# Sparse attention of a hybrid decoder layer: all heads of a query block in turn, logits from 64 rows, division once a block

## The reference

```
h = h + 0.5 * swiglu(rmsnorm(h), ffn1)
h = h + [GLA(4 heads) | sparse attention(8 heads of 64)] @ w_out      # on rmsnorm(h) @ w_in
h = h + 0.5 * swiglu(rmsnorm(h), ffn2)
out = rmsnorm(h)[:, 16:]
```

```
logits = q . k / 8, over the selected keys that are visible, else -inf
p      = softmax(logits)
out    = p @ v                                    # per head
```

## Time and profile before

| | us |
|---|---|
| median of 3 runs | 1195.07 (1193.54 to 1195.66) |
| the profiled execution: its time | 1195.07 |
| the profiled execution: its span | 1195.1 |
| TensorE busy in it | 1147.0 (96%) |
| attention, first logits to first projection matmul | 687.9 to 769.6 |

### The profile page before, as it was taken

The page is one execution under the profiler, slowest core; times in us unless marked ns, Lnnn a source line. Parts: engine busy times, 40 slices in busy tenths (PEclk is TensorE's granted clock), DMA queues, the critical chain, the costliest instruction groups (busy, mean ns, idle before and its releaser), DMA issues.

```text
span 1195.1 us, 19518 instructions
## 1 busy us (share of the span) xinstructions
PE 1147.0 (96%) x7331; PEld 1021.1 (85%) x7331; DVE 620.5 (52%) x989; ACT 359.0 (30%) x547; POOL 508.0 (43%) x283
## 2 busy tenths in 40 slices
PE   6999999999999999995789999999999999999997
PEld 6999999999999996895787777887887888788886
DVE  5644123531346955996996466555542144512556
ACT  5422112221222342621122356533221122212223
POOL 2634444444433635246746150045444444444442
PEclk8999999999999999997989899999999999999999
DMA  5423332333321444132312000033333333333311
GB/s 179 124 88 89 90 93 83 103 90 88 88 70 54 124 129 112 47 105 57 96 36 71 19 1 1 17 89 100 110 89 88 106 88 88 106 88 88 88 53 71
DMA packets 175545, 98.70 MB, mean 83 GB/s; under 512 B 6019, under 2 KB 169910, under 8 KB 175494
## 3 DMA queue, kind: packets, MB, share of 16 engines
q1 hardware_dynamic: 175494, 98.02, 28.5%
HBM read 91.18 MB, written 2.10 MB: 78 GB/s over the span
## 4 chain that ended last, share of the span: by engine, by line
PE 85%; DVE 7%; issue 5%; ACT 1%; POOL 1%; DVEq 0%; POOLq 0%; ACTq 0%
PE ps L1538 70%; PE ps L371 5%; PE ps L540 3%; PE ps L550 2%; PE ps L567 2%; DVE mask L857 1%; PE ps L525 1%; DVE ikga L904 1%; DVE iq L926 1%; POOL wl L1192 1%; PE ps L462 1%; DVE small L853 1%; DVE gb L882 0%; DVE t L904 0%; PE ps L513 0%
## 5 line engine op out<-in xcount | busy, mean ns | idle before, releaser
L1192 POOL TENSOR_TENSOR wl<-raw,wh 128x1024 fp32r<-128x1024 f32 x173 | 429.7, 2486 | 614.0 <-ACT wh L1327 613.8
L1538 PE MATMUL ps<-xh,wh 128*128 128x264 f32 (+2 forms) x1392 | 354.0, 315 | 6.1 <-DVE xl L1436 5.6
L1538 PE MATMUL ps<-xl,wh 128*128 128x264 f32 (+2 forms) x1392 | 353.6, 315 | 0.0
L1538 PE MATMUL ps<-xh,wl 128*128 128x264 f32 (+2 forms) x1392 | 352.2, 314 | 0.0
L1327 ACT ACTIVATE wh<-raw 128x1024 fp32r<-128x1024 f32 x173 | 181.3, 1052 | 289.8 <-PE ps L1538 278.7
L1538 PEld LDWEIGHTS ps<-xh,wh 128*128 128x128 f32 (+1 forms) x1392 | 230.2, 190 | 23.4 <-issue 7.2
L1538 PEld LDWEIGHTS ps<-xl,wh 128*128 128x128 f32 (+1 forms) x1392 | 229.6, 190 | 15.7 <-issue 0.2
L1538 PEld LDWEIGHTS ps<-xh,wl 128*128 128x128 f32 (+1 forms) x1392 | 229.4, 190 | 14.8
L1538 PE MATMUL ps<-ah,wh 128*128 128x264 f32 (+1 forms) x592 | 166.8, 330 | 0.0
L1538 PE MATMUL ps<-al,wh 128*128 128x264 f32 (+1 forms) x592 | 166.4, 330 | 0.0
L1538 PE MATMUL ps<-ah,wl 128*128 128x264 f32 (+1 forms) x592 | 166.1, 329 | 0.0
(11 more groups left out here) (210 smaller groups left out, 1067.0 us busy)
## 6 DMA issues: line engine op xcount, KB each, us to landing
raw<-in_ffn_w_gate SPq DMA_DIRECT2D x44, 512.0 KB, 3.7
raw<-in_ffn_w_up SPq DMA_DIRECT2D x44, 512.0 KB, 3.7
raw<-in_ffn_w_down SPq DMA_DIRECT2D x32, 512.0 KB, 3.8
raw<-in_w_in SPq DMA_DIRECT2D x28, 512.0 KB, 3.7
raw<-in_ffn_w_down SPq DMA_DIRECT2D x16, 384.0 KB, 3.3
raw<-in_w_out SPq DMA_DIRECT2D x8, 512.0 KB, 3.9
sw<-pjb SPq DMA_DIRECT2D x32, 66.0 KB, 2.0
xin<-in_x SPq DMA_DIRECT2D x4, 512.0 KB, 4.2
```

Of the source, the lines that this page charges most:

```text
L1192: pool.tensor_tensor(wl[:, slot, :], raw[:, slot, :], wh[:, slot, :].bitcast(F32), ALU.subtract).then_inc(w_split, 1)
L1538: mm = pe.matmul(ps[0:m, bank + a, 0:width], w[:, slot, k * P:k * P + m], r[:, tiles[k], t:t + width], start=(k == 0 and n == 0), stop=(k ...
```

## The change

- The order of the steps: block 4 first, then 3, 2, 1, 0, all eight heads of a block in turn, written out without a loop (`ATT_ORDER`, `TURNS`).
- Logits: queries and keys are read where the projection left them (`pjb`), 64 rows, even heads on partitions 0 to 63, odd heads on 64 to 127. From step 8 on, those of two steps are issued one after the other. GpSimd's zeroing and its copies (`stage`) go.
- Probabilities: exponential in place in `lg` (four buffers instead of two), without a sum; `dg` and `inverse` go. They are turned by plain transposes against the identity, and copied by VectorE (even steps) or ScalarE (odd steps), in one instruction.
- Values: the turned probabilities are the weights, and a head's 64 value columns with a column of ones, 65, move. The result has queries on partitions and the sum of the exponentials beside them. All eight heads of a block gather in two banks.
- Once a block (`scale_out`): a reciprocal of eight sums and one multiply; TensorE transposes the four tiles back (`turn_out`, after the fourth step of the next block), ScalarE and VectorE split them in `ah` and `al`.
- `values` run two steps behind.

```diff
         def att_step(n):
-            pair, rest = divmod(n, 2 * len(BLK))
-            e, rest = divmod(rest, len(BLK))
-            b = ATT_ORDER[rest]
-            return (pair, e, b) + BLK[b]
+            b = ATT_ORDER[n // HEADS]
+            return (b, n % HEADS) + BLK[b]
+        def qk_bank(n):
+            return 2 * (n % 2) if n < HEADS else n % 4
+        TURNS = []
+        for n_head in range(N_ATT):
+            TURNS.append((True, n_head))
+            if n_head % HEADS == 3 and n_head > HEADS:
+                TURNS.append((False, n_head // HEADS - 1))
+        TURNS.append((False, len(BLK) - 1))
+        def keep_probs(eng, n):
+            b, hd, s, w = att_step(n)
+            t = TURNS.index((True, n))
+            eng.wait_ge(p_turned, n + 1)
+            if n >= 3:
+                eng.wait_ge(pv_done, n - 2)
+            src, dst = ps[:, 4 + t % 2, 0:(b + 1) * w], pt[:, n % 3, 0:(b + 1) * w]
+            if by_dve(n):
+                eng.tensor_copy(dst, src).then_inc(pt_dve, 1)
+            else:
+                eng.activation(dst, src, ACT.Copy).then_inc(pt_act, 1)
@@ TensorE
-            pe.wait_ge(kst_zero, 4)
+            def logits(n):
+                b, hd, s, w = att_step(n)
+                pair, e = hd // 2, HD * (hd % 2)
+                for a, (k0, kn) in enumerate(key_parts(b)):
+                    mm = pe.matmul(ps[0:w, qk_bank(n) + a, 0:kn], pjb[e:e + HD, pair, s:s + w],
+                                   pjb[e:e + HD, 4 + pair, k0:k0 + kn], start=True, stop=True)
+                mm.then_inc(qk_done, 1)
+            def turn_probs(n, t):
+                b, hd, s, w = att_step(n)
+                pe.wait_ge(exp_done, n + 1)
+                if t >= 2:
+                    turn_free(pe, t - 2)
+                for c in range(b + 1):
+                    sc, wc = BLK[c]
+                    mm = pe.transpose(ps[0:wc, 4 + t % 2, c * w:(c + 1) * w], lg[0:w, n % 4, sc:sc + wc],
+                                      ident[0:w, 0:w])
+                mm.then_inc(p_turned, 1)
+            def values(n):
+                b, hd, s, w = att_step(n)
+                probs_kept(pe, n)
+                if hd == 0 and n:
+                    pe.wait_ge(o_scaled, n // HEADS)
+                c0 = (hd % 4) * (HD + 1)
+                for c in range(b + 1):
+                    wc = BLK[c][1]
+                    mm = pe.matmul(ps[0:w, 6 + hd // 4, c0:c0 + HD + 1], pt[0:wc, n % 3, c * w:(c + 1) * w],
+                                   dv_heads[0:wc, c, hd, :], start=(c == 0), stop=(c == b))
+                mm.then_inc(pv_done, 1)
+            def turn_out(i, t):
+                s, w = BLK[ATT_ORDER[i]]
+                pe.wait_ge(o_scaled, i + 1)
+                turn_free(pe, t - 2)
+                for j in range(4):
+                    mm = pe.transpose(ps[:, 4 + t % 2, j * w:(j + 1) * w], onat[0:w, j * P:(j + 1) * P],
+                                      ident[0:w, 0:w])
+                mm.then_inc(n_turned, 1)
+            logits(0)
+            pe.wait_ge(o_normed, 1)
+            logits(1)
+            for t, (is_head, n) in enumerate(TURNS):
+                if not is_head:
+                    if n == len(BLK) - 1:
+                        values(N_ATT - 2)
+                        values(N_ATT - 1)
+                    turn_out(n, t)
+                    continue
+                if n + 2 < HEADS:
+                    pe.wait_ge(lg_done, n + 1)
+                    logits(n + 2)
+                elif n % 2 == 0 and n + 2 < N_ATT:
+                    pe.wait_ge(lg_done, n + 1 if n + 2 == HEADS else n)
+                    logits(n + 2)
+                    if n + 2 == HEADS:
+                        pe.wait_ge(lg_done, n + 2)
+                    logits(n + 3)
+                if n == 0:
+                    pe.wait_ge(o_normed, len(WIN))
+                turn_probs(n, t)
+                if n >= 2:
+                    values(n - 2)
@@ VectorE
+            def scale_out(i):
+                s, w = BLK[ATT_ORDER[i]]
+                o = ps[0:w, 6:8, 0:4 * (HD + 1)].rearrange("p a (h d) -> p a h d", d=HD + 1)
+                r = rinv[0:w, :].rearrange("p (a h) -> p a h", a=2)
+                dve.wait_ge(pv_done, HEADS * (i + 1))
+                dve.reciprocal(r.unsqueeze(3), o[:, :, :, HD:HD + 1]).then_inc(sum_inv, 1)
+                if i:
+                    dve.wait_ge(n_turned, i)
+                dve.wait_ge(sum_inv, i + 1)
+                dve.tensor_tensor(onat[0:w, :].rearrange("p (a h d) -> p a h d", a=2, d=HD), o[:, :, :, 0:HD],
+                                  r.unsqueeze(3).broadcast_to([w, 2, 4, HD]), ALU.mult).then_inc(o_scaled, 1)
+            for is_head, n in TURNS:
+                if is_head:
+                    if n + 2 < N_ATT:
+                        masked(n + 2)
+                    if by_dve(n):
+                        keep_probs(dve, n)
+                    if n % HEADS == 1 and n > HEADS:
+                        scale_out(n // HEADS - 1)
...
@@ ScalarE: the exponential of the next step, then the copy of an odd step, or the outputs' high half
+            for is_head, n in TURNS:
+                if is_head:
+                    if n + 1 < N_ATT:
+                        probs(n + 1)
+                    if not by_dve(n):
+                        keep_probs(act, n)
...
@@ GpSimd
+            pool.memset(dv_heads[:, :, :, HD:HD + 1], 1.0).then_inc(dv_ones, 1)
-            for n, (pair, e) in enumerate(((0, 0), (0, 1), (1, 0), (1, 1))):
-                pool.memset(kst[pair][e][64 * (1 - e):64 * (1 - e) + HD, :], 0.0).then_inc(kst_zero, 1)
-            stage(0)
-            stage(1)
...
-            stage(2)
-            stage(3)
```

More of the change, by code:

```diff
@@ L154, in build @@
         pjb = sb("pjb", [P, 8, TOK])
-        dv = sb("dv", [P, 5, 512])
+        dv = sb("dv", [P, 5, HEADS * (HD + 1)])
         mask = sb("mask", [P, sum(SEEN)])
@@ L531, in pe_mixer @@
             pe.wait_ge(s_new, GLA_HEADS * FULL_WIN)
-            pe.wait_ge(kst_zero, 4)
[L533 to L548, removed]
-                        wc = BLK[c][1]
-                        mm = pe.matmul(ps[HD * e:HD * (e + 1), 6 + n % 2, 0:w], vst[pair][0:wc, c, HD * e:HD * (e + 1)],
-                                       pt[0:wc, n % 2, c * w:(c + 1) * w], start=(c == 0), stop=(c == b))
-                    mm.then_inc(pv_done, 1)
-                logits(0)
-                logits(1)
-                for n in range(N_ATT):
-                    pair, e, b, s, w = att_step(n)
-                    if n + 2 < N_ATT:
-                        logits(n + 2)
-                    if n == 0:
-                        pe.wait_ge(o_normed, len(WIN))
-                    pe.wait_ge(diag_done, at(i, N_ATT, n + 3))
-                    pe.wait_ge(pt_kept, at(i, N_ATT, n + 1))
-                    for c in range(b + 1):
-                        sc, wc = BLK[c]
-                        mm = pe.matmul(ps[0:wc, 4 + n % 2, c * w:(c + 1) * w], pr[0:w, n % 2, sc:sc + wc],
-                                       dg[0:w, n % 2, 0:w], start=True, stop=True)
-                    mm.then_inc(pt_done, 1)
-                    if n:
-                        values(n - 1)
-                values(N_ATT - 1)
@@ new lines, in masked @@
+            def masked(n):
+                b, hd, s, w = att_step(n)
+                dve.wait_ge(qk_done, n + 1)
+                if n >= 4:
+                    dve.wait_ge(p_turned, n - 3)
+                src = ps[0:w, qk_bank(n), 0:SEEN[b]] if SEEN[b] <= 512 else ps[0:w, qk_bank(n):qk_bank(n) + 2, 0:HALF]
+                dve.tensor_tensor_reduce(out=key_view(lg[0:w, n % 4, 0:SEEN[b]], b), in0=src,
+                                         in1=key_view(mask[0:w, MASK_AT[b]:MASK_AT[b] + SEEN[b]], b), scale=-HD ** -0.5,
+                                         scalar=3.0e38, op0=ALU.add, op1=ALU.min,
+                                         accum_out=stat[0:w, n % 4:n % 4 + 1]).then_inc(lg_done, 1)
@@ L1408, in _ @@
             dve.memset(scrap[:, :], 0.0).then_inc(scrap_done, 1)
-            for free in (up_scaled, lg_done, pt_kept, m_lo, diag_done, pv_done):
-                dve.sem_inc(free, 2)
+            dve.sem_inc(up_scaled, 2)
             dve.sem_inc(top_taken, 2)
```

174 lines of the change are left out of this document (56 added, 118 removed).

## The result

The changed kernel takes 1215.63 us (median of 4 runs, 1212.94 to 1220.19) against 1195.37 of the kernel before on the same chip (4 runs, 1193.54 to 1195.78): ratio 1.0181, 95% interval 1.0156 to 1.0207. It is slower; the forecast was 1187.4, faster, with a range of 1183.0 to 1192.5. The profiled execution is the 1212.94 one, with a span of 1211.1.

What follows compares the result with a forecast made beforehand. The prediction took TensorE to bound the kernel: 69.1 us of passes + 1.6 waits + 1.45 tail + 1.8 start = 74.0 against 81.7 for the stage, 7.7 less, so 1195.1 became 1187.4 us, range 1183.0 to 1192.5.

Steps and rivals of the forecast that it cites:

- Start: Attention stage's start: clock at 0.50 until about 691 us loses 1.6 us, with 0.15 of waiting 1.8.
- rival 3: Attention stage: clock sinks to 0.50 because of transposes or 64-row work; low throughout adds 69 us; chance 0.04.
- Turning: Transposes of the probabilities: two passes a chunk, 2.71 us a head, 21.7 for eight; no gain from being transposes.
- Values: Values matmuls: passes priced by their weights, 0.089 us each (0.114 for 128 columns), 21.8 us in all.
- rival 5: Values matmuls priced by their 65 moving columns: 8.4 us less, total 1179; chance 0.05.
- Pairs: Logits from block 3 on: two heads issued together cost as one, 7.3 us; up to 7.3 more otherwise.
- Rival 1: Paired logits overlap not at all or only half: 3.7 or 7.3 us more, 1191 or 1194.6; chance 0.14.
- Switches: Shape changes around 64-row logits: 0.15 + 0.18 us each time in and out, 23 times, 7.6 us.
- Rival 2: Each change between transpose and plain matmul costs 0.16 us, some 56 times: 9 us more, 1196.3; chance 0.06.
- Waits: TensorE stalls at block edges for the division and the outputs' bank, in blocks 1 and 0: 1.6 us together.
- tail: Stage's end, from last turning through last values and division: TensorE idle 1.4 to 1.45 us.
- rival 4: Blocks 1 and 0 become bound by the latency chain: 0.25 us a step in 16 steps, 1191; chance 0.09.

Runs made afterwards that it cites:

- e11: Changed kernel with zero-padded 128-row logits in block 4 alone, 64-row pairs from block 3 on: 1173.27 us, ratio 0.9826.
- e1: Changed kernel with logits over all 128 rows, summing the two heads of a pair (not the reference's numbers): 1177.67 us.
- e5: Kernel before with 64-row logits, nothing else changed: 1272.48 us.
- e14: Changed kernel with 60 transposes of 128x128 put ahead of the first logits: 1223.57 us.
- e6: Kernel before with the probabilities turned by plain transposes, division by the sum left out: 1184.06 us.
- e13: Changed kernel with every transpose of the probabilities issued twice: 1236.25 us.
- e2: Changed kernel with the probabilities turned by plain matmuls against the identity, two passes each: 1202.86 us.
- e10: e8 timed again, 64-row logits always in pairs and 100 moving columns in the values: 1174.16 us, ratio 0.9832.
- e4: Changed kernel with 20 full matmuls (128 rows, 512 columns) put ahead of the first logits: 1218.45 us.
- e7: Changed kernel with logits over 128 rows by zero-padded queries, one copy a head filled by GpSimd: 1171.86 us.
- e9: e7 timed again, changed kernel with zero-padded 128-row logits: 1172.69 us, ratio 0.9819.
- e3: Changed kernel with 128 instead of 65 moving columns in the values: 1192.60 us.
- e8: Changed kernel with 64-row logits always in interleaved pairs, block 4 too, and 100 moving columns in the values: 1176.43 us.
- e15: Changed kernel with 60 transposes of 100x100 put ahead of the first logits: 1225.07 us.

## Why the prediction was wrong

**The step that failed** is the clock of the stage. In the sum it is the term Start: 1.6 us lost, and the clock 1.00 "from about 691"; all of the 69.1 us of passes is priced at full clock. The other way stood there as rival 3, "the clock sinks to 0.50 within the stage because of transposes or of 64-row work", and got 0.04. The runs showed 0.50 from the stage's first instruction to its last, 102.45 us for the 74.0 of the forecast, and with it a sign that the prediction had named, 0.50 after 695 us. Against e11, which differs in block 4's padding alone, the low clock costs 102.45 - 59.98 = 42.5 us. I had the decisive row in hand: the spreading matmuls, 20 rows each, keep TensorE busy 8.41 of 8.70 us at 0.50, while full-row logits see it rise. I read it as a delay of 3 us, not as a property of the work that follows. And the row that made the chance so small, the transposes at the kernel's start, says nothing of 64 rows, and what decides first is the logits' rows (e1, e5). The transposes are not out of it: they raise the clock by themselves (e14) and leave it up beside full rows (e6), but beside 64 rows they didn't bring it up where plain matmuls did (e13, e2).

Rival 3's price, "low throughout adds 69", was too high. Some 14 of the 69.1 are passes that take less than priced (below), and a pass takes not twice as long at half clock but 1.9 times: ten of the values 1.61 us for 0.85. The rest I have not taken apart.

**Turning: mis-sized.** I priced a plain transpose at two passes, because the rows of the kernel before show a matmul as two records and I carried that over. The earlier trace rows had the answer: L1613 and L1633 are x16 for 16 transposes of 128x128. At full clock e11's chain, below, shows five chunks in 0.43 us, 0.087 each, so a head takes 14 x 0.087 + 0.11 = 1.3, eight heads 10.6 instead of 21.7; the outputs' transposes take 0.35 a block instead of 0.71. That is 13 us in the kernel's favour.

The chain of e11, a head of block 4 and a pair in block 3:

```profile
702.63 0.43 PE ps L551 x5
...
703.91 0.90 PE ps L540 x4
704.81 0.49 PE ps L551 x4
705.30 0.85 PE ps L563 x10
706.16 0.35 PE ps L551 x4
706.51 0.85 PE ps L563 x10
```

**Values: right.** 0.85 for ten passes is 0.085 each (forecast 0.089), not the 0.054 of 65 moving columns (rival 5): e10's 100 columns take 1.67 where 65 take 1.61, both at half clock.

**Pairs: right.** 0.90 us for two heads with 428 columns, where one takes 0.89. Rival 1 falls.

**Switches: right.** 0.49 for the first four transposes behind a pair of logits, 0.35 for the next four: 0.14 on that side (forecast 0.15), and the 0.90 is the 0.706 of the columns and 0.19 (forecast 0.18). Between transposes and values there is nothing: 0.35 and 0.85 are the passes alone. Rival 2 falls.

**Waits: right in size.** In e11, at full clock but for its start and end, TensorE idles 59.98 - 57.42 = 2.56 us; forecast 1.6 at block edges and 1.45 in the tail. What its matmuls waited for in e11 (engine, line, what it waited for: us, times, longest), L572 being the outputs' transposes, L563 the values and L551 the transposes of the probabilities:

```profile
PE ps L572 <- DVE onat L1074: 1.1, 1, 1.1
PE ps L563 <- DVE onat L1074: 0.8, 2, 0.5
PE ps L551 <- DVE al L1093: 0.4, 1, 0.4
```

The 0.8 for the multiply at two block edges is the 0.25 and 0.55 of the forecast. No matmul is down as waiting for a mask, an exponential or a copy of probabilities, where rival 4 had 0.25 a step in 16 steps: it falls. In the changed kernel, at half clock, VectorE waits 42.3 us for the logits. What the forecast lacks is the wait for the first mask, 0.92 us where the stage starts at full clock (e4).

The wait in the tail can cost more than its 1.1 us. In e11 the clock falls behind it, and the projection starts at half clock (first row: the stretch behind the wait). In e7 the same wait is there and the clock stays up (second row).

```profile
743.70:747.00 3.30, 3.30 (x10) 2.76 (x11) 0.69 (x1) 1.54 (x2) 0.67 (x1) 0.50 0.03 5
```

```profile
744.60:748.00 3.40, 3.40 (x17) 2.72 (x16) 0.69 (x1) 1.55 (x2) 1.73 (x1) 1.00 0.00 0
```

Of the traces that come to this wait at full clock, e2, e9 and e11 show the fall and e1, e3, e7, e8, e10 and e13 don't. About 3.3 us at half clock cost some 1.6, which is part of the spread of the runs.

Put together at 1.00: 74.0 forecast, less 13.0 for the single-pass transposes and 1.0 for the values, less some 2.3 of switches that e11's padded block 4 saves, makes 57.7; measured 59.98. A granted clock of 0.96 over the stage is 0.04 x 59.98 = 2.4 us lost where the forecast had 1.6, which is 0.8 of the 2.3 left; the other 1.5 I can't place. So but for the clock the sum adds up to within these 1.5 us, and the design is worth more than forecast: some 20 us, which e9, e10 and e11 then give, 1172.7 to 1174.2 against 1194.0. The intervals of the three overlap, so none is shown to be the best. e9 is the simplest: logits over full rows with zeros.

## What to carry to other kernels

Before you take rows, passes or moving columns out of a stage that TensorE bounds, look up at which granted clock it runs and what the stretch with the low clock had been doing; less work in the same busy time can halve the clock, and then every pass left costs nearly double (1.61 us for 0.85 here). If it does, fill the array with something free: zero rows in the operand that is stationary anyway, moving columns up to what loading the weights takes, or a full-row start for work that holds the level it finds. And count a transpose's passes from the rows that show transposes, not from those of matmuls.

## What the runs showed of the hardware that I had not expected

- TensorE stays at half clock while busy with hardly a gap: 26.40 of 26.40 us in the changed kernel, 155.41 of 156.11 in e5. "TensorE: Matmul & The Clock Gate" of the Trainium skill, section on the HAM clock gate, has the clock follow how busy the engine has recently been; busy as the profile counts it was not enough here.
- Rows of zeros count: e7 and e9 rise as e1 does (to 1.00 after 5.07 us in e7, 6.2 in e1).
- The same work holds either level: 375 passes at 0.99 in e11, at 0.50 in the changed kernel.
- A plain fp32 transpose is one pass: 0.087 us for 100 columns at full clock (0.35 for four), 0.168 at half (0.67 for four), and transposes alone raised the clock (e14, e15).
- 64-row matmuls of two heads in different halves of the rows ran side by side in pairs, not only in longer series: 0.90 us for four passes of 428 columns.
- A wait of 1.1 us of TensorE at full clock was followed by a fall to 0.50 in three traces (e2, e9, e11) and by none in six.
